# A two-block model in one launch: paired value products and a sink column in attention, a filter stage on 128 rows with its norm applied in the convolutions

## The reference

```
h = jnp.sin(fr1 * (z @ w1 + b1))
h = jnp.sin(fr2 * (h @ w2 + b2))
h = (h @ w3).astype(jnp.float32).reshape(l, HYENA_ORDER, 2, B_WIDTH)
...
h = h * window[:, None, None, :]
kern = jnp.concatenate([h[:, :, 0], jnp.flip(h[:, :, 1], axis=0)], axis=0)
return kern / (jnp.sum(jnp.abs(kern), axis=0, keepdims=True) + HYENA_L1_EPS)
...
z = gate * (fft_conv(z, kern[:, o]).astype(z.dtype) + hy_bias[o] * z)
```

```
s = jnp.broadcast_to(sink.astype(jnp.float32).reshape(ATT_KV_HEADS, ATT_GROUP, 1, 1),
                     scores.shape[:-1] + (1,))
p = jax.nn.softmax(jnp.concatenate([s, scores], axis=-1), axis=-1)
return p[..., 1:]
```

## Time and profile before

| what | value |
|---|---|
| time, median of 3 runs | 3637.28 us (3632.05 to 14180.58) |
| the profiled execution | 3641.72 us, span 3639.8 us |
| granted PE clock, mean | 0.964 |
| PE busy | 3382.8 us (93%) |
| DVE busy | 2028.8 us (56%) |
| ACT busy | 1147.9 us (32%) |
| POOL busy | 129.5 us (4%) |

### The profile page before, as it was taken

The page is one execution under the profiler, slowest core; times in us unless marked ns, Lnnn a source line. Parts: engine busy times, 40 slices in busy tenths (PEclk is TensorE's granted clock), DMA queues, the critical chain, the costliest instruction groups (busy, mean ns, idle before and its releaser), DMA issues.

```text
span 3639.8 us, 49244 instructions
## 1 busy us (share of the span) xinstructions
PE 3382.8 (93%) x18408; PEld 2921.0 (80%) x18408; DVE 2028.8 (56%) x3181; ACT 1147.9 (32%) x1540; POOL 129.5 (4%) x64
## 2 busy tenths in 40 slices
PE   5799999999989989999988889999999989899998
PEld 2399999988778778887777668999999767678887
DVE  5756342548856558874468464654433466653334
ACT  1221211345531133224333263311212342543222
POOL 2100000000000000000111100000000111100000
PEclk9999999999999999999989799999999988999999
DMA  5334332421122235553200201333322211113232
GB/s 199 107 116 139 116 139 70 140 68 36 42 99 73 94 116 173 190 179 103 83 26 24 76 1 50 107 132 123 131 93 69 75 39 35 47 47 98 90 100 92
DMA packets 101862, 339.95 MB, mean 93 GB/s; under 512 B 10287, under 2 KB 21423, under 8 KB 100240
## 3 DMA queue, kind: packets, MB, share of 16 engines
q1 hardware_dynamic: 82760, 301.90, 24.8%
q10 hardware_dynamic: 18952, 36.01, 2.8%
HBM read 323.71 MB, written 14.16 MB: 93 GB/s over the span
## 4 chain that ended last, share of the span: by engine, by line
PE 76%; DVE 13%; ACT 5%; issue 3%; DMA 2%; ACTq 0%; POOL 0%; DVEq 0%; SPq 0%
PE ps L424 61%; PE ps L466 4%; PE ps L1034 2%; PE ps L450 2%; ACT pr L2263 1%; DVE u_P L1192 1%; PE ps L1724 1%; PE ps L1010 1%; DMA raw<-in_mod_stream 1%; PE ps L1711 1%; ACT pT L2272 1%; PE ps L2199 1%; DVE u_Z L1176 1%; DMA hyena_k<-fst 1%; PE ps L1051 1%
## 5 line engine op out<-in xcount | busy, mean ns | idle before, releaser
L517 ACT ACTIVATE wr_hi<-raw 128x1024 fp32r<-128x1024 f32 x388 | 411.7, 1061 | 603.7 <-PE ps L424 551.0
L527 DVE TENSOR_TENSOR wr_lo<-raw,wr_hi 128x1024 fp32r<-128x1024 f32 x348 | 426.2, 1225 | 99.9 <-ACT wr_hi L517 69.1
L424 PE MATMUL ps<-xx_hi,wr_hi 128*128 128x512 f32 x1056 | 418.4, 396 | 0.5 <-ACT ff_gate L842 0.4
L424 PE MATMUL ps<-xx_lo,wr_hi 128*128 128x512 f32 x1056 | 414.1, 392 | 0.0
L424 PE MATMUL ps<-xx_hi,wr_lo 128*128 128x512 f32 x1056 | 413.7, 392 | 0.0
L890 DVE TENSOR_TENSOR ff_raw<-ps,ff_gate 128x768 f32<-128x768 f32 (+1 forms) x88 | 72.6, 824 | 576.8 <-PE ps L424 571.6
L424 PE MATMUL ps<-xa_hi,wr_hi 128*128 128x384 f32 x1344 | 341.1, 334 | 0.0
L424 PE MATMUL ps<-xa_lo,wr_hi 128*128 128x384 f32 x1344 | 340.9, 334 | 0.0
L424 PE MATMUL ps<-xa_hi,wr_lo 128*128 128x384 f32 x1344 | 340.9, 334 | 0.0
L571 DVE CUSTOM_DVE_ANT_0 ps<-raw,cb 128x1024 f32<-128x1024 f32 x240 | 295.3, 1230 | 52.9 <-DMA raw<-in_mod_stream 37.0
L424 PE MATMUL ps<-hid_hi,wr_hi 128*128 128x384 f32 (+1 forms) x1056 | 316.2, 353 | 4.1 <-DVE hid_lo L897 2.1
(11 more groups left out here) (396 smaller groups left out, 5367.9 us busy)
## 6 DMA issues: line engine op xcount, KB each, us to landing
raw<-in_stream SPq DMA_DIRECT2D x392, 512.0 KB, 3.5
raw<-in_mod_stream SPq DMA_DIRECT2D x168, 512.0 KB, 4.4
hK<-hyena_k ACTq DMA_DIRECT2D x4, 1152.0 KB, 6.1
h_kept<-H ACTq DMA_DIRECT2D x2, 2048.0 KB, 9.1
hyena_k<-fst ACTq DMA_DIRECT2D x14, 256.0 KB, 10.5
H<-in_h ACTq DMA_DIRECT2D x1, 3072.0 KB, 15.8
h_kept<-H ACTq DMA_DIRECT2D x1, 3072.0 KB, 11.1
H<-h_kept ACTq DMA_DIRECT2D x1, 3072.0 KB, 9.9
```

The costliest lines, as they stand in the source:

```text
L424: last = pe.matmul(gslot(slot)[:, col:col + n], w, rhs[part], start=(bi == 0 and pi == 0), stop=(bi == len(blocks) - 1 and pi == 2))
L517: act.activation(wr_hi[:, s, :], raw[:, s % RAW, :], ACT.Copy).then_inc(tile_hi, 1)
L527: dve.tensor_tensor(wr_lo[:, s, :], raw[:, s % RAW, :], wr_hi[:, s, :], ALU.subtract).then_inc(tile_lo, 1)
```

## The change

In attention the sink becomes column 0 of `sl`: one Exp with its sum covers it, the Exp at L2266 and the addition at L2345 go, and DVE copies the sink into the column at qb 0 for each head. `pr` is then scaled and transposed from column 1 on. The value products of both heads of a pair are issued together, alternating between the heads, after the turn of the first item of the next pair; `pT` has four buffers. In the filter stage the forward and reversed positions lie on partitions 0 to 63 and 64 to 127, so that an array of 1024 columns becomes one of 512. The sum of absolute values is formed as columns: `fabs` is the weight and two columns of ones move, 8 products a tile t. DVE keeps only 4 numbers per partition and order: `hy_gain` = 1/(sum + eps), and `hy_skip` = (sum + eps) times `hy_bias`; they are applied in the Hyena stage, and the filters are stored as they come. ACT copies the convolution results from PSUM to `fst` itself and waits for the buffer's earlier stores. `third` is issued by ACT behind the second sine. The squares of H are taken for o = 0.

```diff
@@ pe_filters
-                last = pe.matmul(m[0:64, h * NX:(h + 1) * NX], fw1[:, :], fz[:, h * NX:(h + 1) * NX],
+                last = pe.matmul(m[h * HD:(h + 1) * HD, 0:NX], fw1[:, :], fz[:, h * NX:(h + 1) * NX],
...
-                            last = pe.matmul(m[:, h * NX:(h + 1) * NX], fh[:, 1, h * NX + t * P:h * NX + (t + 1) * P],
-                                             fw3[:, 2 * o + h, :], start=True, stop=True)
+                            f = slice(h * HD, (h + 1) * HD)
+                            last = pe.matmul(m[:, h * NX:(h + 1) * NX], fh[f, 1, t * P:(t + 1) * P],
+                                             fw3[f, o, :], start=True, stop=True)
...
-                            last = pe.matmul(gslot(norm)[:, 0:NX], ones[:, :], fabs[:, (t - 1) % 2, h, :],
-                                             start=(t == 1 and h == 0), stop=(t == 4 and h == 1))
+                            for g in range(4):
+                                last = pe.matmul(gslot(norm)[:, 2 * g:2 * g + 2], fabs[:, (t - 1) % 2, h, g * P:(g + 1) * P],
+                                                 ones[:, 0:2], start=(t == 1 and h == 0 and g == 0), stop=(t == 4 and h == 1),
+                                                 skip_group_check=True)
@@ act_filters
-            for dst, src in third:
-                act.dma_start(dst, src).then_inc(third_landed, 16)
...
+            for dst, src in third:
+                act.dma_start(dst, src).then_inc(third_landed, 16)
             for o in range(2):
...
                 for c in range(NFREQ):
-                    tally.take("misc_done")
-                    act.wait_ge(misc_free[tally.place("misc_done", 1)], tally.read("misc_done"))
-                    if o:
-                        act.wait_ge(pos_ready, tally.next("pos_ready"))
-                        act.wait_ge(ssq_step, tally.next("ssq_step"))
-                        act.activation(first_squares[0][:, 0, :], H[:, c, :], ACT.Square).then_inc(sq_ready, 1)
                     st = fst[:, c % 4, :]
+                    ms = tally.take("misc_done")
+                    act.wait_ge(misc_done, tally.now("misc_done"))
+                    if n:
+                        act.wait_ge(k_stored[c % 4], n)
+                    act.activation(st, mslot(ms)[:, 0:NX], ACT.Copy).then_inc(misc_free[ms], 1)
...
+                    if not o:
+                        act.wait_ge(pos_ready, tally.next("pos_ready"))
+                        act.wait_ge(ssq_step, tally.next("ssq_step"))
+                        act.activation(first_squares[0][:, 0, :], H[:, c, :], ACT.Square).then_inc(sq_ready, 1)
@@ dve_filters
-                dve.tensor_scalar(fnorm[:, :], gslot(norm)[:, 0:NX], 1e-6, None, ALU.add)
-                dve.reciprocal(fnorm[:, :], fnorm[:, :])
+                norms = hy_skip[:, 4 * o:4 * o + 4]
+                dve.tensor_scalar(norms, gslot(norm)[:, 0:8:2], 1e-6, None, ALU.add)
+                dve.reciprocal(hy_gain[:, 4 * o:4 * o + 4], norms)
+                dve.tensor_tensor(norms, norms, vec("hy_bias", 4 * o, 4), ALU.mult)
...
-                    dve.tensor_tensor(fst[:, c % 4, :], mslot(ms)[:, 0:NX], fnorm[:, :], ALU.mult
+                    tally.passed("misc_done")
@@ dve_hyena
-                        dve.tensor_tensor(v, v, hv[:, 2, :], ALU.mult).then_inc(z_done, 1)
+                        dve.scalar_tensor_tensor(out=v, in0=v, scalar=gain, in1=hv[:, 2, :], op0=ALU.mult,
+                                                 op1=ALU.mult).then_inc(z_done, 1)
@@ pe_attention
+                for n, kc in enumerate(keys):
+                    for s in range(2):
+                        f = slice(s * HD, (s + 1) * HD)
+                        last = pe.matmul(gslot(0)[f, qb * P:(qb + 1) * P], avt[:, kc, f],
+                                         pT[:, (2 * p + s) % 4, n * P:(n + 1) * P], start=(n == 0),
+                                         stop=(n == len(keys) - 1), skip_group_check=True)
...
+            for p in range(pairs):
+                if p + 1 < pairs:
+                    scores(p + 1)
+                turn(2 * p)
+                if p:
+                    values(p - 1)
+                turn(2 * p + 1)
@@ act_attention
-                act.activation(pr[:, i % 2, 0:n], sl[:, i % 2, 0:n], ACT.Exp, bias=low, scale=-1.0,
-                               accum_out=sums[:, 0:1]).then_inc(act_step, 1)
-                act.wait_ge(act_step, tally.next("act_step"))
-                act.activation(sums[:, 1:2], mx[:, h, 2:3], ACT.Exp, bias=low, scale=-1.0).then_inc(exp_ready, 1)
+                act.activation(pr[:, i % 2, 0:n + 1], sl[:, i % 2, 0:n + 1], ACT.Exp, bias=small[:, w + 1:w + 2],
+                               scale=-1.0, accum_out=small[:, w + 2:w + 3]).then_inc(exp_ready, 1)
@@ dve_attention
+                if qb == 0:
+                    dve.tensor_copy(sl[:, i % 2, 0:1], sink).then_inc(dve_step, 1)
...
-                dve.tensor_tensor(small[:, w + 5:w + 6], small[:, w + 2:w + 3], small[:, w + 3:w + 4], ALU.add
-                dve.reciprocal(small[:, w + 5:w + 6], small[:, w + 5:w + 6]).then_inc(dve_step, 1)
+                dve.reciprocal(small[:, w + 5:w + 6], small[:, w + 2:w + 3]).then_inc(dve_step, 1)
```

More of the change, by code:

```diff
@@ L200, in build @@
         fw1 = arena("fw1", [64], 1024, parts=33)
[L201 to L204, removed]
+        fw2 = arena("fw2", [64], 1088)
+        fw3 = arena("fw3", [2, 512], 1152)
+        fh = arena("fh", [2, NX], 3200)
+        fk = arena("fk", [NX], 5248)
+        hy_gain, hy_skip = small[:, 32:40], small[:, 24:32]
         fwin = arena("fwin", [2, 4, 512], 6272)
@@ L1320, in pe_filters @@
             for h in range(2):
-                last = pe.matmul(m[0:64, h * NX:(h + 1) * NX], fw2[:, :], fh[:, 0, h * NX:(h + 1) * NX],
+                f = slice(h * HD, (h + 1) * HD)
+                last = pe.matmul(m[f, 0:NX], fw2[f, :], fh[f, 0, :],
                                  start=True, stop=True)
@@ L1470, in dve_filters @@
                 dve.wait_ge(abs_summed, tally.next("abs_summed", 4))
-                dve.tensor_scalar(fnorm[:, :], gslot(norm)[:, 0:NX], 1e-6, None, ALU.add).then_inc(slot_free[norm], 1)
+                norms = hy_skip[:, 4 * o:4 * o + 4]
+                dve.tensor_scalar(norms, gslot(norm)[:, 0:8:2], 1e-6, None, ALU.add).then_inc(slot_free[norm], 1)
                 dve.wait_ge(slot_free[norm], tally.read("group"))
-                dve.wait_ge(slot_free[tally.place("group", 1)], tally.read("group", 1))
-                dve.reciprocal(fnorm[:, :], fnorm[:, :]).then_inc(dve_step, 1)
+                dve.reciprocal(hy_gain[:, 4 * o:4 * o + 4], norms).then_inc(dve_step, 1)
+                dve.wait_ge(dve_step, tally.next("dve_step"))
+                dve.tensor_tensor(norms, norms, vec("hy_bias", 4 * o, 4), ALU.mult).then_inc(dve_step, 1)
                 dve.wait_ge(dve_step, tally.next("dve_step"))
@@ L1481, in dve_filters @@
                         dve_mod_bias(dve, tally, bias, o * NFREQ + c - 3, 2)
-                    ms = tally.take("misc_done")
-                    dve.wait_ge(misc_done, tally.now("misc_done"))
-                    stored = K_STORES[c % 4]
-                    times = o * 2 + (c >= 4)
-                    want = 16 * (sum(stored) * (times // 2) + (stored[0] if times % 2 else 0))
-                    if want:
-                        dve.wait_ge(k_stored[c % 4], want)
-                    dve.tensor_tensor(fst[:, c % 4, :], mslot(ms)[:, 0:NX], fnorm[:, :], ALU.mult
-                        ).then_inc(misc_free[ms], 1)
-                    dve.wait_ge(misc_free[ms], tally.read("misc_done"))
+                    tally.passed("misc_done")
         def pe_values(pe, tally, count, vt, order=None):
@@ L2213, in turn, with values @@
                 tally.passed("pt_done")
-            def values(i):
-                c, s, qb = items[i]
-                if i == len(items) - 1:
-                    pe.wait_ge(pt_ready, tally.next("pt_ready"))
-                if (s, qb) == (0, 0) and c:
+            def values(p):
+                c, _, qb = items[2 * p]
+                if qb == 0 and c:
                     pe.wait_ge(mix_ready, tally.next("mix_ready"))
                 keys = key_blocks(qb)
-                f = slice(s * HD, (s + 1) * HD)
                 for n, kc in enumerate(keys):
-                    last = pe.matmul(gslot(0)[f, qb * P:(qb + 1) * P], avt[:, kc, f],
-                                     pT[:, i % 2, n * P:(n + 1) * P], start=(n == 0), stop=(n == len(keys) - 1),
-                                     skip_group_check=True)
-                if i == len(items) - 1 or items[i + 1][0] != c:
+                    for s in range(2):
[3 more added lines that the diff above has]
+                                         stop=(n == len(keys) - 1), skip_group_check=True)
+                if 2 * p + 2 == len(items) or items[2 * p + 2][0] != c:
                     last.then_inc(ao_done, 1)
@@ L2232, in pe_attention @@
```

(20 more changed lines are left out.)

40 lines of the change are left out of this document (20 added, 20 removed).

## The result

| | before | after |
|---|---|---|
| time, median | 3634.78 us (4 runs: 3632.05, 3632.29, 3637.28 and 14180.58) | 3594.84 us (3593.62 to 3598.92, 4 runs) |
| profiled execution | 3641.72 us, span 3639.8 | 3593.62 us, span 3591.7 |
| first product of L450 | 168.40 us | 163.56 us |
| attention, first layer, scores to last values | 124.7 us | 100.3 us |
| attention, second layer | 88.3 us | 78.2 us |

The ratio is 0.9889, 95% interval 0.9874 to 0.9903: 40 us faster (35 to 46). The forecast was 3586 with a range of 3565 to 3607; it holds, but its two terms were 30 and 23 us, and the profile shows 34.4 for attention (24.3 + 10.1) and only 4.8 for the filter stage. The two spans differ by 48.1.

What follows compares the result with a forecast made beforehand. PE carries 76% of the span, 61% in untouched tile matmuls, so only stretches it doesn't bind can give. Attention 30 plus filter 23 saves 53 of 3641.7: 3588.7, or 3586 on the median's footing, range 3565 to 3607.

Steps and rivals of the forecast that it cites:

- The filter term: Filter stage: PE reaches L450 at 144 instead of 168.4, saving 23 us; bounds 14 and 36.
- the attention term: Both attention stages: sink column and alternated values save 30 us, 19 in the first and 11 in the second.
- (c): Attention: scaling `pr` from column 1 on costs zero; the other end was 11 us.
- (d): Attention: value products of two heads, alternated, overlap and take 1.3 us instead of 2.6; other end 2.4.
- rival 2: Attention: value products don't overlap, PE binds and attention gives only 10 us, total 3606; chance 0.08.
- The ten slow pairs: Attention: some 10 of 40 pairs stay PE-bound at half clock, at starts and changes of c, saving 0.7 each.
- (e): Filter stage: eight ACT loads moved behind the second sine let PE start the filter rows at 28.5 instead of 38.2.
- (f): Filter summing loops: with the narrow norm, 14 us from first window to last sum at full clock, 19 for the first.
- (g): Filter convolution loops: 127-row stores and the blocked issues behind them make a loop 33 to 34 us.
- 1: Filter stage and attention: stores don't bind and attention gives everything, 74 us or more saved, 3564 or below; chance 0.12.
- 3: Attention and filter stage: thinner PE work drops its clock to 1.2 GHz, 30 to 35 us slower, 3670; chance 0.04.
- (h): Hyena: eight products get a scalar, costed at nothing, at most 1.4 us.

Runs made afterwards that it cites:

- e5: Kernel before with the attention part of the change alone, filter stage as before: 3605.84 us, ratio 0.9911 to the kernel before.
- e6: Kernel before with the sink as a key column alone, value products in their old order and place: 3616.66 us, ratio 0.9949 to the kernel before.
- e2: Changed kernel with the norm's sums taken with 128 columns of ones instead of 2: 3588.89 us, ratio 0.9875 to the kernel before.
- e3: Changed kernel with each 127-row store cut in two and 128 columns of ones: 3568.59 us, ratio 0.9818 to the kernel before.
- e10: Changed kernel with 127-row stores cut, 128 columns of ones and squares of H back in the second convolution loop: 3562.52 us, ratio 0.9789 to before.
- e1: Changed kernel with each 127-row store cut into rows 16 to 127 and 1 to 15: 3578.00 us, ratio 0.9838 to the kernel before.
- e7: Changed kernel with the two heads' value products issued head after head in their new place: 3599.90 us, ratio 0.9905 to the kernel before.

## Why the prediction was right, step by step

The range held, for a sum in which one term was 2 to 4 us too small and the other 15 to 19 too large. The filter term (4 to 8 us measured) fell below its own lower bound of 14; that the total lay inside all the same was in part luck: the attention term came out above its 30, and a range of 42 us took up the rest. The centre also had 1.7 us with no term behind it: 3588.7 less 4.4 is 3584.3, not 3586.

**Attention: right in size and mechanism.** 30 us (19 + 11) against 34.4 (24.3 + 10.1) by the stages and 32 (25 to 40) by e5. (c) costs zero: 490 ns median against 487. By the rule of the Trainium skill (VectorE: DVE Perf Modes, Mode 2×_2P) zero was due, and the trace agrees. (d) 1.31 us for both heads, as taken from L616. Where PE was thought the bound "without (d)", giving 10 us, e6 shows 17.4: that rival was mis-sized. Most pairs still gained, by 0.16 to 0.84 where PE had run at full clock, and two at a change of c by 1.3 and 2.0. And rival 2, values one head after the other, would have cost 4 to 8 us, not 20 (3606 - 3586): in the new place they overlap in part even so, and the place gives most of (d). The ten slow pairs I had allowed were fewer: from the second head pair on, the pairs at a change of c take 5.0 in both layers (6.6 to 7.4 before in the first, 5.3 to 6.2 in the second).

**Filter stage: the mechanism right, its sizes not.** The chain through the two 127-row stores came as forecast, and (e) was right within a microsecond (second sine's products at 29.15, forecast 28.5). The points:

| | forecast | after | lost |
|---|---|---|---|
| first convolution | 47.5 | 53.6 | 6.1 |
| second summing loop | 82 | 93.4 | 5.3 more |
| convolution 0 | 96.5 | 113.2 | 5.3 more |
| its store issued | 101.5 | 119.5 | 1.3 more |
| landed | 119 | 137.6 | 0.6 more |
| PE's L450 | 144 | 163.6 | 1.0 more |

The step that failed is (f), "I take 14 us from the first window to the last sum when the clock is full, 19 for the first loop", with its 16 instructions "1.8 us; its other uses show 0.2, 3.3 us". The clock wasn't full. The second loop took 19.8 us (93.4 to 113.2), because three of its four groups took 3.5 us in place of 1.95 and the products between them 2.0 in place of 1.08; with 128 columns (e2) the sums are back at 2.05 and the first loop ends at 47.1, the 47.5 of the forecast. I had read L601's 0.11 us as the price of the form and the 0.2 as an odd case. The second was the price at half clock: those uses, 24 in 5.28 us from 2022.4 on in the kernel before, lie in a stretch granted 0.50. And the narrow form doesn't end that state. The bound "14 if PE falls to half clock in its waits" put the cause in the waits, not in the sums themselves, and its 14 was still 6 to 10 too much.

(g): half-clocked products lengthen the first convolution loop by 2.6 at convolution 0 and 3.1 at convolution 7 (6.13 and 6.59 against 3.5), and the second by 1.8 and 2.8 (5.26 and 6.29). The blocked issue was put at 5.5 and was 6.2 and 8.9. Little of the second loop's loss is left at the end: I had taken the way from its long store to L450 from the trace of before, 25 us, and it was 26. What wasn't in the sum at all: DVE's mod products at 2162 ns beside GpSimd (e3) where the earlier trace rows has 1230. In the changed kernel (1661) the store hides it; it costs once the store is mended. "The squares now lie in the first loop; each is an ACT op of 0.8 and fits" was nearly true of ACT (one of 0.85 stands in the chain, at 85.26), and forgot that GpSimd adds each one up beside DVE. The forecast bound of 36 "if the stores don't bind" (132.5) is where e3 (136.6) and e10 (130.4) lie.

**The rivals.** 1 fell: the stores bind (e1). 3 fell in attention, where the stages were granted 0.93 and 0.91 (before 0.89 and 0.94); in the filter stage, which it also named, half clock did cost (10.4 us of L450 by e2), though through the narrow sums and not through thinner waits. (h) can't be told from zero: from the first L450 to the one that follows Hyena and its GLA it was 1573.3 us (168.40 to 1741.69) and is 1573.7 (163.56 to 1737.29).

## What to carry to other kernels

A store of 127 rows took 16 to 18 us here, where those of 128, 112 and 15 rows in e1 landed within 6.1: cut such a row count before anything is put behind it (18 us here for three lines). Before an instruction is made narrower to save PE time, ask what clock PE has there and whether the narrow form lets it rise; work that costs the same at the full clock may keep the clock low. When products of several heads wait on the same engine, try grouping them at one place first: here the place gave 13 us, the order within the group 4 to 8.

## What was not expected of the hardware

PE was busy for 20.0 of 20 us (e1, 90 to 110), up to 106.8 with products of two and of 512 columns in turn, and the granted clock stayed at 0.50; with 128 columns in their place it was 0.85 and 1.00 (e3). The Trainium skill (TensorE: Matmul & The Clock Gate, What's actually happening) says that activity releases the lower level; here a PE without a gap, as the profile counts it, stayed at the lower one. Issues behind a slow store on ACT's queue blocked for 3.8 to 8.9 us; once the store was cut (e1) the one at block 4 took 0.3. DVE's products took 2.85 us beside one of GpSimd's sums and 1.23 right after the last (e3). And twenty value products in two runs of ten take 1.95 us where nothing stands between the two (e7), and 2.48 where something does (e6); the reason wasn't tried.
